# A hybrid diffusion step on one core: two token chunks, the first one's expert gather beside the second one's front

## What is computed

```
h = rmsnorm(x) * (1 + scale1) + shift1            # scale, shift, gate from silu(cond) @ w_ada
f, conv, q, k, v, ..., gates = split(h @ w_in)
y = four mixers (Fourier, convolution, full attention, windowed attention)
merged = sum over b of sigmoid(gates_b + b_gate_b) * (y_b @ w_b)
x = x + g1 * (merged @ w_out)
h = rmsnorm(x) * (1 + scale2) + shift2
q = h @ w_q ; scores against 2 x 128 sub-keys for 8 heads
16 best of each half, 16 best of the 256 pairs -> 8 x 16 = 128 experts per token
u, v = u_tab[expert], v_tab[expert]               # tables of 16384 rows
x = x + g2 * sum(softmax(score) * gelu(u . h) * v)
```

## Time and profile before

| what | value |
|---|---|
| median of 3 runs | 6026.77 us |
| the profiled execution | 6025.39 us, span 6023.6 us |
| mean granted TensorE clock | 0.889 |
| busy: TensorE, VectorE, ScalarE, GpSimd | 4699.7, 3560.7, 845.4, 1569.8 us |
| DMA | 1509.72 MB, of it 1342.26 MB by GpSimd's indirect queue |

### The profile page before, as it was taken

The page is one execution under the profiler, slowest core; times in us unless marked ns, Lnnn a source line. Parts: engine busy times, 40 slices in busy tenths (PEclk is TensorE's granted clock), DMA queues, the critical chain, the costliest instruction groups (busy, mean ns, idle before and its releaser), DMA issues.

```text
span 6023.6 us, 46241 instructions
## 1 busy us (share of the span) xinstructions
PE 4699.7 (78%) x15008; PEld 2671.4 (44%) x15008; DVE 3560.7 (59%) x7774; ACT 845.4 (14%) x2368; POOL 1569.8 (26%) x1310
## 2 busy tenths in 40 slices
PE   5999999896666666666669999998966666666665
PEld 3766677772222222222237666777622222222222
DVE  0655311148888888886507452111588888888765
ACT  1023200101111111111110332001011111111111
POOL 0000000004444444445400000000044444444453
PEclk8999999998888888888889999999988888888887
DMA  6100011109999999999851000111199999999996
GB/s 235 56 28 1 22 63 59 61 29 377 421 411 421 410 421 414 422 417 422 332 212 49 29 1 32 58 65 49 39 421 421 410 421 413 422 411 421 421 422 289
DMA packets 213697, 1509.72 MB, mean 251 GB/s; under 512 B 24656, under 2 KB 26960, under 8 KB 37072
## 3 DMA queue, kind: packets, MB, share of 16 engines
q0 software_dynamic: 184320, 1342.26, 53.8%
q1 hardware_dynamic: 29136, 164.52, 7.5%
HBM read 1503.54 MB, written 3.15 MB: 250 GB/s over the span
## 4 chain that ended last, share of the span: by engine, by line
PE 47%; DMA 37%; DVE 10%; ACT 2%; issue 2%; POOL 1%; DVEq 1%; SPq 0%; ACTq 0%; POOLq 0%
DMA B<-tables,R 23%; PE ps L633 9%; DMA A<-tables,R 8%; PE ps L710 7%; PE ps L465 5%; PE ps L638 5%; DMA R<-tables,R 5%; PE ps L690 4%; DVE B L1242 3%; DVE hT L1274 3%; PE ps L450 2%; PE ps L652 2%; DMA B<-ws 2%; PE ps L570 2%; PE ps L557 2%
## 5 line engine op out<-in xcount | busy, mean ns | idle before, releaser
L710 PE MATMUL ps<-B,hT 128*128 128x512 f32 x2752 | 1590.7, 729 | 764.5 <-ACT hT L905 764.5
L392 POOL DMA_INDIRECT B<-tables,R x908 | 1098.4, 1210 | 2775.2 <-DVE A L1231 1609.9
L710 PEld LDWEIGHTS ps<-B,hT 128*128 128x128 f32 x2752 | 621.5, 233 | 1702.5 <-ACT hT L905 930.6
L1242 DVE SCALAR_TENSOR_TENSOR B<-B,M 128x1024 f32<-128x1024 f32 x908 | 1096.0, 1224 | 317.7 <-DMA B<-tables,R 292.7
L710 PE MATMUL ps<-A,hT 128*128 128x512 f32 x864 | 534.7, 756 | 268.1 <-ACT hT L905 268.1
L633 PE MATMUL ps<-hT,B 128*128 128x320 f32 x2048 | 561.9, 433 | 1.4 <-ACT R L864 1.4
L633 PEld LDWEIGHTS ps<-hT,B 128*128 128x128 f32 x2048 | 389.2, 190 | 164.6 <-ACT R L864 3.0
L710 PEld LDWEIGHTS ps<-A,hT 128*128 128x128 f32 x864 | 202.3, 243 | 576.7 <-ACT hT L905 325.1
L392 POOL DMA_INDIRECT A<-tables,R x272 | 333.7, 1227 | 364.8 <-PE ps L710 276.9
L899 ACT ACTIVATE T<-T 128x4 f32<-128x4 f32 x320 | 65.7, 205 | 2412.3 <-DVEq L1244 2412.3
L1242 DVE SCALAR_TENSOR_TENSOR A<-A,M 128x1024 f32<-128x1024 f32 x272 | 332.9, 1225 | 117.2 <-DMA A<-tables,R 108.2
(11 more groups left out here) (207 smaller groups left out, 4855.6 us busy)
## 6 DMA issues: line engine op xcount, KB each, us to landing
B<-ws SPq DMA_DIRECT2D x96, 1024.0 KB, 5.1
B<-ws SPq DMA_DIRECT2D x64, 768.0 KB, 4.1
B<-tables,R POOLq DMA_INDIRECT x908, 17.9
R<-tabs SPq DMA_DIRECT2D x2, 2176.0 KB, 8.5
A<-tables,R POOLq DMA_INDIRECT x272, 20.7
x<-xin SPq DMA_DIRECT2D x1, 2560.0 KB, 9.1
y<-M SPq DMA_DIRECT2D x1, 2560.0 KB, 7.9
R<-tables,R POOLq DMA_INDIRECT x100, 18.5
```

The lines of the kernel that those rows point to most:

```text
L392: pool.indirect_dma_start(out=ring[HOME[n]], out_offset=None, in_=tables[:, :], in_offset=bass.IndirectOffsetOnAxis(ap=EI[:, n:n + 1], axi ...
L710: mm = pe.matmul(ps[:, bk + c, :], diag[p % DIAGS], v_row[:, c * 512:(c + 1) * 512], start=(gt == 0 and i == 0), stop=(gt == GROUPS - 1 an ...
L1242: v.scalar_tensor_tensor(out=u_row, in0=u_row, scalar=1.0, in1=h2[:, n // SLOTS, :], op0=ALU.mult, op1=ALU.mult, accum_out=dots[:, n % (2 ...
```

## The change

Everything from the merge on runs in two *chunks*: chunk 0 is tiles 0 and 1, chunk 1 tiles 2 to 4 (`CHUNKS`). Chunk 0 goes through merge, output, norm, rows and keys alone. Then chunk 1 goes through the same steps, and the expert groups of tiles 0 and 1 are written between them on TensorE, ScalarE and VectorE (`MG_STEP`, `OUT_STEP`, `KEY_STEP`): two groups in each merge step, one in each quarter of an output tile, six around the norm, two in each of 16 key steps. What is left, 14 groups of tile 1 and tiles 2 to 4, follows alone.

- The 44 weight blocks of merge, output and keys are loaded once for each chunk (`AGAIN`).
- A group of tiles 0 and 1 has two rows, one for TensorE and one for VectorE, in the later part both for TensorE; tiles 2 to 4 keep groups of four.
- The ring starts with 5 places and gets more at rows 40, 132, 236, 352, 400 and 528 (`LATER`), 15 in the end. GpSimd starts with tile 0's first head.
- Tile 0's last four heads and tile 1's are picked between chunk 1's merge steps, tile 2's between its key steps.
- ScalarE, not VectorE, copies the key scores; one query block of two or three tiles fits a PSUM bank, and the order of query and score products is that of the new banks.
- The merge's sigmoid is written as 0.5 (1 + tanh(x / 2)), the half folded into the residual gates.
- The first norm needs only blocks 0 to 7 of the modulation; it is written between the other blocks, and the second part of the modulation follows it. The Fourier tables are loaded after the 24 modulation blocks instead of ahead of them.
- The gate products stand between chunk 0's merge steps.
- Attention: VectorE divides the probabilities before the transpose; four heads are transposed side by side, and the values (64 columns) are the stationary weights while 256 columns of probabilities move, two halves of the array for two pairs of heads. The result comes out transposed, so the transposes at the tile's end go.

The core of the diff (the rest follows from it):

```diff
+CHUNKS = ((0, 1), (2, 3, 4))
-RING = 10
-NG = 4
-PE_G = 3
+RING = 5
+GROUPS = [Group(t, n, size, size - 1 + (164 <= n < 2 * SLOTS and (n % 4 == 2 or n >= 228))) for t in range(TILES)
+          for size in ((2, 4)[CHUNK[t]],) for n in range(t * SLOTS, (t + 1) * SLOTS, size)]
+MG_STEP = 2
+OUT_STEP = 4
+KEY_STEP = 2
+LATER = {40: (5,), 132: (6,), 236: (7, 8, 9, 10, 11), 352: (12,), 400: (13,), 528: (14,)}
...
# SP
+                    sp.wait_ge(w_used.sem, w_used.at(l, n if n in range(BLOCKS, BLOCKS + WS) else
+                                                     AT_OP + AGAIN if n in range(AT_OP + AGAIN, AT_OP + AGAIN + WS) else n + 1 - WS))
...
# GpSimd
-                pool.wait_ge(pq_s.sem, pq_s.at(l, UNITS))
-                for n in range(N_GROUPS * NG):
+                for n in range(TILES * SLOTS):
+                    s, b = HOME[n], BEFORE[n]
...
+                    elif s == 3:
+                        pool.wait_ge(pq_s.sem, pq_s.at(l, UNITS))
...
# TensorE
+                modulation(0)
+                first_norm(0)
+                first_norm(1)
+                modulation(1)
+                modulation_columns(0)
...
+                    for i in range(nb):
+                        for odd in range(2):
+                            last = pe.matmul(ps[odd * HD:odd * HD + HD, 6 + g % 2, 0:2 * P], V[:, block, c:c + HD],
+                                             pt[:, i, 2 * odd:2 * odd + 2, :], start=(i == 0), stop=(i == nb - 1))
...
+                for s in range(N_MG):
+                    mix_gates(l, 0, s)
+                    mix_branch(l, 0, s)
+                    if s % 4 == 1:
+                        gate_rows(s // 4)
...
+                for s in range(N_MG):
+                    mix_gates(l, 1, s)
+                    experts(l, s * MG_STEP)
+                    mix_branch(l, 1, s)
+                    experts(l, s * MG_STEP + 1)
...
+                for hp in range(UNITS):
+                    queries(l, 1, hp)
+                    if hp:
+                        key_scores(l, 1, hp - 1)
+                    experts(l, AT_KEYS + hp * KEY_STEP)
+                    experts(l, AT_KEYS + hp * KEY_STEP + 1)
...
# ScalarE
+                act.activation(SG[s % 2][:, 0:w], ps[:, s % 2 * 2, 0:w], ACT.Tanh, bias=bgh[:, l, b * KD + j:b * KD + j + 1],
+                               scale=0.5).then_inc(mg_sg.sem, 1)
+                for s in range(N_MG):
+                    experts(l, s * MG_STEP)
+                    sigmoid(l, 1, s)
+                    experts(l, s * MG_STEP + 1)
...
# VectorE
+                        probs = Pb[e][:, 0:blocks(t, u) * P]
+                        v.tensor_scalar(out=probs, in0=probs, scalar1=sm[:, 4, e:e + 1], scalar2=None, op0=ALU.mult)\
+                            .then_inc(a_p.sem, 1)
...
+                def experts(q):
+                    g = GROUPS[q]
+                    products(q)
+                    if g.tile and g.place == len(g.slots):
+                        residual(g.tile - 1)
+                    if q:
+                        sums(q - 1)
+                    if g.place in OPENS[g.tile]:
+                        gates(g)
+                    weights(q)
...
+                for s in range(N_MG):
+                    if s:
+                        mix(1, s - 1)
+                    experts(s * MG_STEP)
+                    if s < UNITS:
+                        select(*divmod(2 * PH + 2 * s, 4 * PH))
+                    experts(s * MG_STEP + 1)
+                    select(*divmod(2 * PH + (2 * s + 1 if s < UNITS else UNITS + s), 4 * PH))
```

More of the change, by code:

```diff
@@ new lines, in norm_transposes, with experts @@
+            def norm_transposes(l, t, at, xs, bk, free):
+                pe.wait_ge(n_xs.sem, n_xs.at(l, at + 1))
+                if free is not None:
+                    pe.wait_ge(n_ht.sem, n_ht.at(l, free + 1))
+                for k in range(KD):
+                    last = pe.transpose(ps[:, bk + k // 4, (k % 4) * P:(k % 4 + 1) * P], xs[:, k * P:(k + 1) * P], ident)
+                last.then_inc(n_tp.sem, 1)
+            def experts(l, q):
+                g = GROUPS[q]
+                bk = 4 + (g.tile % 2) * 2
+                if g.place == 0 and g.tile >= 2:
+                    pe.wait_ge(tile_done.sem, tile_done.at(l, g.tile - 1))
+                for n in g.pe:
+                    v_row = ring[HOME[n]][:, D:ROW]
+                    pe.wait_ge(diag_ok.sem, diag_ok.at(l, PE_AT[n] + 1))
+                    for c in range(2):
+                        mm = pe.matmul(ps[:, bk + c, :], diag[PE_AT[n] % DIAGS], v_row[:, c * 512:(c + 1) * 512],
+                                       start=(n % SLOTS == 0), stop=(PE_AT[n] + 1 == PE_BY[g.tile]))
+                    mm.then_inc(pe_used.sem, 1)
@@ new lines, in transposes @@
+                        pe.wait_ge(a_pa.sem, a_pa.at(l, u0 + p))
+                        pe.wait_ge(a_pd.sem, a_pd.at(l, u0 + p))
+                        for i in range(blocks(t, u)):
+                            bank, o = (4, i) if i < split else (5, i - split)
+                            last = pe.transpose(ps[:, bank, o * P:(o + 1) * P], Pb[p % 2][:, i * P:(i + 1) * P], ident)
+                        last.then_inc(a_t.sem, 1)
+                    for p in range(UNITS + 1):
+                        if p < UNITS:
+                            scores(p)
+                        if p:
+                            transposes(p - 1)
+                        if p in (5, 9, 13):
+                            values(n, t, p // 4 - 1)
@@ L1305, in _ @@
+                score_copy(1, UNITS - 1)
+                v.drain()
+                for q in range(AT_END, N_GROUPS):
+                    experts(q)
+                    g = GROUPS[q]
+                    if g.tile == 1:
+                        select(2, 2 * UNITS - 5 + q - AT_END)
+                    elif g.tile in (2, 3):
+                        select(g.tile + 1, g.place // 4)
+                sums(N_GROUPS - 1)
+                residual(TILES - 1)
                 v.drain().then_inc(layer_done.sem, 1)
@@ L1320, in windowed @@
     return u < HEADS
+ORDER = [0, 1, 2, 3, 8, 9, 10, 11, 4, 5, 6, 7, 12, 13, 14, 15]
+SIDE = [p % 2 * 2 + p % 4 // 2 for p in range(UNITS)]
 def blocks(t, u):
```

1023 lines of the change are left out of this document (562 added, 461 removed).

## The result

The changed kernel takes 5666.0 us (median of 4 runs, 5663.9 to 5673.2) against 6028.4 us before: a ratio of 0.9404, 95% interval [0.9387, 0.942]. Forecast were 5550 us in a range of 5310 to 5870. The time lies in the range, and the saving is 362 us of the 475 forecast.

A forecast was written before the change was run, and what follows sets the result against it. The prediction took a front without DMA and a DMA-only gather, one after the other, as the bound. Layer 0 would end at 927.6 + 787 + 1057 = 2771.6 instead of 3007.8 us; 6025.4 - 472 gave 5550 us, range 5310 to 5870.

The forecast's parts named there:

- main term: Whole layer: the front that wants no DMA overlaps the DMA-only gather; layer 0 ends 236 us earlier, 472 in two layers.
- Attention: Attention stretch: cheaper value products on TensorE, mostly taken back by the new chain through VectorE; gain 10 us.
- The end of -40: Lower end of the attention's gain range, -40 to +30 us.
- First norm: Between last modulation product and first convolution product: 30.8 us shrink to 7, a gain of 24, from 0 to 31.
- Merge of chunk 1: Chunk 1's merge beside the gather: 233 us for steps 0 to 15, 208 for 16 to 31, 20 more, 461 us.
- The 20 us for ring and late blocks: Chunk 1's merge: 20 us more for a five-place ring at first and second to fourth weight blocks that wait.
- VectorE is the bound: Chunk 1's merge steps 0 to 15: VectorE 14.6 us a step, above TensorE 11.2 and DMA 11.9; 233 us.
- Three bounds within a few per cent wait for each other: Chunk 1's merge steps 16 to 31: VectorE, DMA and TensorE nearly equal; 13.0 us a step, 208 us.
- DMA alone: Rival: DMA alone sets chunk 1's stretch, 664 us instead of 787; 5305 us in all; chance 0.15.
- Turns: Rival: TensorE and VectorE alternate, 5.2 us exposed in each merge step, 166 a layer; 5885 us; chance 0.17.
- Ring: Rival: too few ring places for chunk 1's 228 rows, 284 us a layer more; 6120 us; chance 0.06.
- Tables: Rival: ScalarE loads tables as gelu and tanh alternate in the merge, 164 us exposed; 5715 us; chance 0.09.

The follow-up runs named there:

- the run with filler: Changed kernel plus a never-read matmul of 256 columns in each of 64 units a layer, where TensorE waits for scaled probabilities: 5585.3 us.
- the run with the norm last: Version with both, the first norm's transposes and scalings put after the whole modulation again: 5560.3 us.
- version with both: Changed kernel with the attention of the kernel before and the first four weight blocks of chunk 1's merge loaded early: 5515.7 us.
- the run with thin blocks: Version with both, chunk 1's merge weights loaded at 192 of 1536 columns, so output differs: 5498.6 us.
- the run with neither: Version with both, tile 1's picking and the full width of chunk 1's merge weights left out, so output differs: 5444.4 us.

## Why the prediction was right, and which term was wrong

*Direction and main term: right, and shown.* The forecast's reason, a front without transfers beside a gather that is nothing else, gives 293 us a layer; without it the kernel is slower than before.

*Attention: the mis-sized term.* The step said "Gain 10 us, from -40 to +30: the new chain through VectorE takes back most of what TensorE loses." It was a loss of 67 in layer 0 and of 50 in layer 1. The sum weighed busy times, 93 us of TensorE against 66 and 40 of VectorE, at the full clock. It named the wait that the change adds (transposes for the scaling) and did not ask what follows on TensorE while it waits: gaps of up to 1.9 us, and a clock of 0.73 for the work around them. With the filler, which brings the full clock, the four tiles take 238 us against the old attention's 230, inside the bounds; the other 57 (295 - 238; 38 in layer 1) come with the clock. On TensorE the value product did get cheaper, close to the better of the two figures (65.7 and 33 us for five tiles): at the full clock its 292 records in the run with filler are busy 35.8 us, so its two halves run side by side, where before's four tiles had 576 records in 84.8 us. The end of -40 was no bound, because it held the clock at the 0.95 of the earlier trace rows. The text did list "an attention stretch longer than 271 us" as what would show it wrong, and the last four tiles alone took 295. The Trainium skill (TensorE: Matmul & The Clock Gate, section "A second HAM failure mode: psum-queue depth-cycling") tells of a kernel in which frequent short idling between groups of matmuls makes the clock oscillate between its two levels; this trace agrees (0.50 and 0.96 in neighbouring windows), and that rule, which spoke against this change, was not weighed.

*First norm: 39.4 instead of 24.* The stretch behind the last modulation product went from 30.8 to 4.5 us (91.4 to 95.9), a gain of 26, close to the forecast's 24; by the run with the norm last, 16 to 22 us of it are the order. The other 13 were not counted: that product itself ends at 91.4 instead of 104.5. No run takes these 13 apart, and the other runs with this head start the convolution between 2 us earlier and 4.5 us later, so a part may be the one execution's. In the trace TensorE's first product comes at 20.7 us instead of 27.0, where the change has moved the Fourier tables' load of 2176 KB behind the modulation's blocks on SP's queue; the remaining 7 are shorter waits for blocks along the way.

*Merge of chunk 1: right in sum and in its steps.* The version with both has no late blocks. ScalarE's tanh of its steps 0, 16 and 31:

```profile
930.02 0.58 ACT L860 ACTIVATE A<-ps,bgh 128x384 f32<-128x384 f32 x1 [1.04 <-PE ps L490]
1161.92 0.56 ACT L860 ACTIVATE A<-ps,bgh 128x384 f32<-128x384 f32 x1
1354.53 0.58 ACT L860 ACTIVATE A<-ps,bgh 128x384 f32<-128x384 f32 x1 [0.49 <-PE ps L490]
```

That is 231.9 / 16 = 14.5 us a step (14.6 forecast) and 192.6 / 15 = 12.8 (13.0). The 20 us for ring and late blocks were the blocks alone, 16 to 25 by the runs: the steps with five places (0 to 9, 14.3 us each) are no longer than the next six with six places (14.8). "VectorE is the bound" for steps 0 to 15 is borne out by the run with thin blocks, and "Three bounds within a few per cent wait for each other", for the steps after them, fits the run with neither.

*The other signs.* In chunk 1's front VectorE is busy 636 of 807 us, 79% where over 85% was listed. The gather's landing in the front's first 200 us is 6.6 to 7.9 us in the three buffers, under 10 as listed, and in layer 0 of the version with both VectorE waits for rows only from merge step 16 on.

*The rivals.* DMA alone: not reached; its floor of 664 us took 417 GB/s, and in chunk 1's front the share of 0.90 to 0.94 moves 349 to 366. Turns: none of 5.2 us a step beside the forecast's sum. Ring: fell with the steps above. Tables: fell. In the changed kernel's merge window, 990 to 1475 us, the tanh stands 32 times between gelus, and all loads are at the three exponentials and the gelus behind them:

```profile
L840 ACT ACTIVATE A<-ps,bgh 128x384 f32<-128x384 f32 x32 | 18.3, 571 | 42.3 <-PE ps L487 42.2
L880 ACT ACTIVATE T<-T 128x2 f32<-128x2 f32 x67 | 13.6, 203 | 289.2 <-DVEq L1445 289.1
L877 ACT ACT_TABLE_LOAD x3 | 3.8, 1283 | 0.1
L880 ACT ACT_TABLE_LOAD x3 | 3.8, 1283 | 0.1
```

No load belongs to the tanh. The list of sets in the Trainium skill (ScalarE: Activation LUTs, section "Table sets: the hidden batching unit") keeps the gelu by tanh out of the set of gelu and does not say which set has it. So the prediction's "by that rule the loads will be there" went further than that list, and the rival rested on a guess.

## What to carry to other kernels

A change that shortens TensorE's work and puts another engine into its chain is to be summed with the gaps it makes: here 28 us of waits came with a clock of 0.73, a filler that brought the full clock made the same four tiles 57 us shorter, and its 64 useless matmuls a layer were worth 81 us. Leaving the attention as it was would have been worth more, 108 us. Before two operations of an in-order engine are exchanged, ask what each one's operand waits for; the earlier one may need work that the later one was to release. Where two halves of a layer load different engines, interleaving them pays even if no engine's work gets less, and what bounds the interleaved part can change within it: here VectorE in the merge's first half, none alone in the second.

## What the runs showed of the hardware that was not expected

- TensorE's granted clock fell to 0.50 around waits of at most 1.9 us and came back while the slower work left hardly any gaps (5.00 us busy of 5), and so on through four tiles of the same program.
- In the attention's four tiles a filler of 256 columns in each unit went with a clock of 1.00 and 0.99 (layers 0 and 1), one of 128 columns with 0.82 and 0.85, none with 0.73 and 0.77, or 0.77 in both layers of another kernel with the same attention. With the large filler 19 waits of up to 1.5 us were still there.
- The same program's attention took 608 and 592 us to the merge in the two layers of one execution.
- The tanh and the gelu by tanh alternated 32 times in 485 us without a table load between them.
- Weight blocks and gathered rows together kept the DMA engines at a share of 0.90 to 0.97 with 349 to 375 GB/s; the rows alone had 410 at 0.99.
